# Stacked scores and DMA placing of rotated parts in the second and third branch of a three-mixer trunk

## What is computed

```python
ang = positions[:, :, None, None] * inv_freq
cos, sin = jnp.cos(ang), jnp.sin(ang)
t1, t2 = t[..., :half], t[..., half:]
return jnp.concatenate([t1 * cos - t2 * sin, t2 * cos + t1 * sin], axis=-1)
...
s = jnp.einsum('bqhmd,bkhmd->bhmqk', qi, k) * scale       # head size 64
prob = jax.nn.softmax(jnp.where(mask, s, NEG), axis=-1)
```

## Time and profile before

| | |
|---|---|
| Median of 3 runs | 1538.78 us (1537.62 to 1540.23) |
| The profiled execution's own time | 1537.43 us |
| Its span, first to last instruction | 1535.6 us |
| Busy: PE, PEld (weight loads) | 1496.2 us (97%), 1203.1 (78%) |
| Busy: DVE, ACT, POOL | 936.3 (61%), 634.8 (41%), 74.4 (5%) |
| Mean granted clock of TensorE | 0.997 |
| Bytes moved by DMA | 129.50 MB |

### The profile page before, as it was taken

One profiled execution on the slowest core, in us unless ns is written; L12 is line 12 of the kernel. 1 busy time (PEld: TensorE's weight loads), 2 busy tenths in 40 slices (PEclk: granted clock), 3 DMA queues, 4 the chain that ended last, 5 costly groups with the idle time before them and its releaser, 6 DMA issues.

```text
span 1535.6 us, 22532 instructions
## 1 busy us (share of the span) xinstructions
PE 1496.2 (97%) x7957; PEld 1203.1 (78%) x7957; DVE 936.3 (61%) x2197; ACT 634.8 (41%) x1499; POOL 74.4 (5%) x80
## 2 busy tenths in 40 slices
PE   8999999999999999999999999999999999999997
PEld 6777777777787777888787787787887877778885
DVE  6866755655557766454576667655555567754544
ACT  6434434333344444343444334334334444434343
POOL 1000000000000010000100000000000000000011
PEclk9999999999999999999999999999999999999998
DMA  7233322222223332332342334222222233233321
GB/s 198 83 83 90 97 76 62 56 70 62 69 63 96 91 82 83 103 105 71 106 108 69 103 83 112 60 53 66 63 62 76 69 96 88 71 101 98 89 86 72
DMA packets 250302, 129.50 MB, mean 84 GB/s; under 512 B 45691, under 2 KB 245973, under 8 KB 250197
## 3 DMA queue, kind: packets, MB, share of 16 engines
q1 hardware_dynamic: 250196, 128.13, 31.4%
HBM read 118.67 MB, written 2.10 MB: 79 GB/s over the span
## 4 chain that ended last, share of the span: by engine, by line
PE 87%; DVE 7%; ACT 3%; issue 2%; DMA 0%; SPq 0%; ACTq 0%; DVEq 0%
PE D L744 24%; PE D L746 22%; PE D L745 22%; PE Ob L932 7%; PE S L891 5%; PE T L910 4%; DVE w_lo L1299 2%; ACT w_hi L1062 1%; PE Mb L948 1%; ACT probs L1178 1%; DVE v_b L1394 1%; PE Mb L858 1%; PE Ob L936 1%; PE Mb L825 1%; DMA raw<-in_w_in_dram 0%
## 5 line engine op out<-in xcount | busy, mean ns | idle before, releaser
L744 PE MATMUL D<-h_hi,w_hi 128*128 128x512 f32 x1264 | 544.5, 431 | 10.1 <-DVE zs L1450 3.8
L746 PE MATMUL D<-h_lo,w_hi 128*128 128x512 f32 x1264 | 496.4, 393 | 0.0
L745 PE MATMUL D<-h_hi,w_lo 128*128 128x512 f32 x1264 | 494.4, 391 | 0.0
L1299 DVE TENSOR_TENSOR w_lo<-raw,w_hi 128x512 fp32r<-128x512 f32 (+2 forms) x504 | 293.0, 623 | 295.1 <-ACT w_hi L1062 294.8
L1062 ACT ACTIVATE w_hi<-raw 128x512 fp32r<-128x512 f32 (+2 forms) x504 | 262.8, 569 | 292.3 <-PE D L746 290.0
L744 PEld LDWEIGHTS D<-h_hi,w_hi 128*128 128x128 f32 x1264 | 238.3, 189 | 71.3 <-issue 20.5
L1178 ACT ACTIVATE probs<-probs,nmax 128x128 f32<-128x128 f32 (+3 forms) x256 | 142.0, 556 | 361.4 <-DVE nmax L1551 361.3
L746 PEld LDWEIGHTS D<-h_lo,w_hi 128*128 128x128 f32 x1264 | 237.2, 188 | 53.2
L745 PEld LDWEIGHTS D<-h_hi,w_lo 128*128 128x128 f32 x1264 | 239.3, 189 | 30.3 <-issue 0.5
L1551 DVE CUSTOM_DVE_ANT_0 probs<-S,maskb 128x128 f32<-128x128 f32 (+3 forms) x256 | 115.1, 487 | 45.6 <-PE S L891 28.7
L542 DVE COPY pT<-T 128x128 f32<-128x128 f32 (+3 forms) x160 | 77.6, 487 | 61.5 <-PE T L910 60.8
(11 more groups left out here) (245 smaller groups left out, 1491.7 us busy)
## 6 DMA issues: line engine op xcount, KB each, us to landing
raw<-in_w_in_dram SPq DMA_DIRECT2D x124, 512.0 KB, 3.9
raw<-in_w_in_dram SPq DMA_DIRECT2D x32, 256.0 KB, 3.7
raw<-in_w_out_dram SPq DMA_DIRECT2D x16, 512.0 KB, 4.2
raw<-in_w_ple_gate_dram SPq DMA_DIRECT2D x16, 512.0 KB, 4.3
rs<-rx SPq DMA_DIRECT2D x80, 64.0 KB, 2.0
raw<-in_cmp_w_k_dram SPq DMA_DIRECT2D x8, 512.0 KB, 3.7
raw<-in_cmp_w_v_dram SPq DMA_DIRECT2D x8, 512.0 KB, 3.8
raw<-in_w_br_a_dram SPq DMA_DIRECT2D x16, 256.0 KB, 2.9
```

Of the source, the lines that this page charges most:

```text
L744: pe.matmul(o, w_hi[:, sl, cs], hi[:, k, :], start=(k == 0), stop=False)
L745: pe.matmul(o, w_lo[:, sl, cs], hi[:, k, :], start=False, stop=False)
L746: ins = pe.matmul(o, w_hi[:, sl, cs], lo[:, k, :], start=False, stop=last)
L1299: TT(w_lo[:, sl, half], raw[:, ring(L, t, RAW), half], f(w_hi[:, sl, half]), ALU.subtract).then_inc(M["dve_lo"], 1)
```

## The change

**Scores.** In B and C the two parts of a query head are stacked: `q_st[b][h]` holds hi on one half of the partitions and lo on the other, and the keys hold each part twice, once on each half. One matmul over 128 rows then gives q_hi·k + q_lo·k for one part of k, and two of them a whole score (with lo·lo, which was left out before). A block is four matmuls over 128 rows where it was six over 64. A's scores stay as they were. TensorE now waits for the maxima of the two heads singly.

**Placing.** The rotation's result no longer goes straight to the arena. The sum is kept in `rc` and the swapped copy in `rs`, which lie side by side as `rcs`: POOL multiplies in place in `rs`, ScalarE writes hi over `rs`, VectorE writes lo over `rc`. A new item `put`, 12 groups behind the tile's end (17 for `kwb`), lets SyncE copy the parts to their places with four DMAs: queries 64 x 512 each, keys 64 x 1024. For it SyncE waits for the lo part, and for the scores that used the place (for `kwb` the hidden layer's last tile, whose input lay there). TensorE waits for the placing at a unit's first scores. The next rotation's swap waits for the last placing.

**Moves.** VectorE's x · cos stands in `rot` and no longer at `end`. `vsb`, `kwb` and `za 3` change places in the fourth stage. The value block `vbd` has memory of its own and is cleared once at the start by POOL.

```diff
-    st[3] = [("qb", 0), ("w1v", 0), ("kwb", 0), ("w1v", 1), ("za", 3), ("w1v", 2), ("vsb", 0), ("w1v", 3), ("vwb", 0)]
+    st[3] = [("qb", 0), ("w1v", 0), ("vsb", 0), ("w1v", 1), ("kwb", 0), ("w1v", 2), ("za", 3), ("w1v", 3), ("vwb", 0)]
...
                 follow.append([11, ("rot", t)])
+                follow.append([17 if kind == "kwb" else 12, ("put", t)])
...
+        def places(kind, n):
+
+            if kind[0] == "q":
+                return [(q_st[n % 2][h][half((h + part_) % 2), :], rcs[half(h), part_ * S:(part_ + 1) * S])
+                        for h in range(2) for part_ in range(2)]
+            at = {"ksb": KS, "kwb": KW, "kc": KC[n % 2]}[kind]
+            return [(part(at + 2 * h, 2)[half(g), :], rcs[half(h), :]) for h in range(2) for g in range(2)]
+
+        def place(M, eng, t):
+
+            kind, n, _ = tiles[t]
+            eng.wait_ge(M["qk_s"], rots.after(t))
             if kind == "kwb":
-                return kw_hi, kw_lo, None
...
+                eng.wait_ge(M["pe_dense"], tile_of[("w1v", 3)] + 1)
+            elif kind != "ksb":
+                eng.wait_ge(M["pe_s"], rows_before[(4 if kind == "qb" else 8) + n - 1])
+            for dst, src in places(kind, n):
+                eng.dma_start(f(dst), src).then_inc(M["put_s"], 16)
...
                             if n > 1:
-                                sp.wait_ge(M["pool_rot"], n - 1)
+                                sp.wait_ge(M["put_s"], put_before[tiles[it[1]][:2]])
...
-                            pool.tensor_tensor(rb[:], rs[:], sinT[:], ALU.mult).then_inc(M["pool_rot"], 1)
...
+                            pool.tensor_tensor(rs[:], rs[:], sinT[:], ALU.mult).then_inc(M["pool_rot"], 1)
...
+                            else:
+                                at = {"c": KC[u % 2], "sel": KS, "win": KW}[m]
+                                for h in range(2):
+                                    pe.wait_ge(M["dve_max"], r - 1 + h)
+                                    qx = q_st[b][h][:, qs]
+                                    pe.matmul(Sc[h][:, 0:n], qx, part(at + 2 * h)[:, 0:n], start=True, stop=False)
+                                    pe.matmul(Sc[h][:, 0:n], qx, part(at + 2 * h + 1)[:, 0:n], start=False, stop=True).then_inc(M["pe_s"], 1)
...
                             dve.wait_ge(M["pool_rot"], r)
+                            TT(rc[:], (qf if tiles[t][0] == "qb" else rx)[:], cosT[:], ALU.mult).then_inc(M["dve_rm"], 1)
                             dve.wait_ge(M["dve_rm"], r)
-                            TT(rc[:], rc[:], rb[:], ALU.add).then_inc(M["dve_rs"], 1)
+                            TT(rc[:], rc[:], rs[:], ALU.add).then_inc(M["dve_rs"], 1)
                             dve.wait_ge(M["act_rot"], r)
-                            TT(lo_, rc[:], f(hi_), ALU.subtract).then_inc(M["qk_s"], 1)
+                            TT(new_lo, rc[:], rs[:], ALU.subtract).then_inc(M["qk_s"], 1)
```

More of the change, by code:

```diff
@@ L309, in hybrid_trunk @@
                 hids.add(kind)
-        elif it[0] == "rot":
-            qk_ready.add(tiles[it[1]][:2])
+        elif it[0] == "put":
+            placed.add(tiles[it[1]][:2])
         elif it[0] in ("vt", "gates", "ht", "kcmp", "vcmp", "cs", "ct", "Y"):
@@ L401, in hybrid_trunk, with half @@
         w_lo = sb("w_lo", [P, SPL, 8 * P], F32R)
-        at_arena = -(-nc.sbuf_base // 32) * 32
         arena = sb("arena", [P, 16 * S], F32R)
-        vbd = nc.alloc_sbuf_tensor_at("vbd", [P, 2, P], F32, offset=at_arena + 12 * S * 4)
         def part(n, k=1):
             return arena[:, n * S:(n + k) * S]
-        q_hi, q_lo = [part(0), part(1)], [part(2), part(3)]
-        k_hi, k_lo = [part(4), part(5)], [part(6), part(7)]
-        ks_hi, ks_lo, kw_hi, kw_lo = part(8), part(9), part(10), part(11)
+        def half(h):
+            return slice(HD * h, HD * h + HD)
+        q_hi, q_lo = [part(0), part(2)], [part(1), part(3)]
+        k_hi, k_lo = [part(4), part(6)], [part(5), part(7)]
+        q_st = [[part(2 * b + h) for h in range(2)] for b in range(2)]
+        KC, KS, KW = (4, 8), 8, 12
         flat_both = part(12, 4).rearrange("p (m c) -> p m c", m=16)
@@ L645, in _ @@
                             static_load(it[1] + 6)
+                        if it[0] == "put":
+                            place(M, sp, it[1])
                     sp.wait_ge(M["dve_ysplit"], 12)
@@ L885, in _ @@
                             n = (i + 1) * P
                             qs = slice(i * P, n)
-                            for step, (qx, kx) in enumerate(((q_hi[b], ka), (q_lo[b], ka), (q_hi[b], kb))):
-                                last = step == 2 and m != "a"
-                                for h in range(2):
-                                    ps = slice(HD * h, HD * h + HD)
-                                    ins = pe.matmul(Sc[h][:, 0:n], qx[ps, qs], kx[ps, 0:n], start=(step == 0), stop=last)
-                                    if last:
-                                        ins.then_inc(M["pe_s"], 1)
@@ L894, in _ @@
-                            if m == "a":
-                                for h in range(2):
-                                    ps, hh = slice(HD * h, HD * h + HD), 2 * u + h
+                            if m == "a":
+                                if r >= 2:
+                                    pe.wait_ge(M["dve_max"], r)
+                                for step, (qx, kx) in enumerate(((q_hi, k_hi), (q_lo, k_hi), (q_hi, k_lo))):
+                                    for h in range(2):
+                                        pe.matmul(Sc[h][:, 0:n], qx[b][half(h), qs], kx[b][half(h), 0:n], start=(step == 0), stop=False)
+                                for h in range(2):
+                                    ps, hh = half(h), 2 * u + h
@@ L1166, in _ @@
                             kind, n, s = tiles[t]
-                            hi_, lo_, u = rot_dst(kind, n)
                             act.wait_ge(M["dve_rs"], rots.after(t))
-                            if u is not None and u >= 2:
-                                act.wait_ge(M["pe_s"], rows_before[u - 1])
-                            A(hi_, rc[:], ACT.Copy).then_inc(M["act_rot"], 1)
+                            A(new_hi, rc[:], ACT.Copy).then_inc(M["act_rot"], 1)
                         elif what == "S":
@@ L1450, in _ @@
                                 STT(zs[:], th[:, slot, :], 1.0, Db[:], ALU.add, ALU.mult).then_inc(done, 1)
-                            elif kind in ROTATED:
-                                r = rots.after(t)
-                                dve.wait_ge(M["act_evac"], act_evac.after(t))
-                                if r > 1:
-                                    dve.wait_ge(M["qk_s"], r - 1)
-                                TT(rc[:], (qf if kind == "qb" else rx)[:], cosT[:], ALU.mult).then_inc(M["dve_rm"], 1)
                             elif kind in ("kcb", "vcb"):
```

59 lines of the change are left out of this document (25 added, 34 removed).

## The result

The changed kernel takes 1547.55 us (median of 4 runs, 1546.13 to 1548.74), the kernel before 1539.51 beside it (4 runs, 1537.62 to 1540.61). The ratio is 1.0056, 95% interval 1.0044 to 1.0068: **slower by 0.56%**, where 1519 us and a gain were forecast.

A forecast was written before the change was run, and what follows sets the result against it. The prediction took TensorE as the bound (87% of the chain that ended last). Scores −21.7 and moved multiply +2.4 made −19.3 us, from a median of 1538.8 to 1519.5, stated as 1519 us; range 1511 to 1528.

The forecast's parts named there:

- the placings: Four more DMAs a rotation on SyncE's queue: off TensorE's path, 8 us against 2.5 + 2.5, no cost.
- the moved multiply: VectorE's cosine product in the rotation: two fourth-stage waits grow by 0.6 us each, 2.4 us in two layers.
- the reordering: Fourth stage's new tile order: taken at nothing; 2.6 us more without the half tile's cover, 5.4 less at best.
- The scores: Second and third branch on TensorE: four 128-row matmuls for six 64-row ones save 21.7 us.
- Rivals 1 and 2: Score blocks: all (1556 us, chance 0.04) or half (1536 us, chance 0.05) of the 0.4 us stays.
- the 0.4 us: TensorE's 64-row score blocks: about this much of each is not streaming, at entry, exit and inside.
- rival 1: Score blocks: the 0.4 us belong to leaving the stream, not to 64 rows; 1556 us, slower, chance 0.04.
- Rival 4: TensorE stands at a stage's first scores for a placing; 28 rotations at 1 us each, 28 us; chance 0.02.
- Rival 3: Rotations: placing lands after 3.5 us, the 1.0 us spare is gone, VectorE stands still; 1523 to 1535 us, chance 0.10.
- The clock: Second and third branch: a lower granted clock was listed as a sign of being wrong, with no size.
- Clearing of the value block: At the start on POOL, ahead of the first data: taken as free.
- weight loads behind the placings: SyncE's queue: loads wait 2.46 us behind the placings' issue; 22 us ahead cover 2.5 + 3.9.

The follow-up runs named there:

- e5: The kernel before with only VectorE's product with the cosine moved from the tile's end into the rotation; 1547.47 against 1538.13 us, ratio 1.0058.
- e6: The kernel before with only the fourth stage's tiles in the new order; 1541.84 against 1537.79 us, ratio 1.0021.
- e4: The changed kernel with queries placed unstacked and six 64-row matmuls a score block again; 1561.80 us against 1538.13 for the kernel before, ratio 1.0148.
- e10: The changed kernel with the third branch's swap, rotation and placing three groups earlier; 1573.26 us against 1537.79 for the kernel before, ratio 1.0225.
- e8: The changed kernel with the cosine product back at the tile's end for all 14 rotations; 1533.36 us against 1537.79 for the kernel before, ratio 0.9968.
- e14: The changed kernel with the third branch's swap, rotation and placing two groups earlier; 1545.78 us against 1537.74 for the kernel before, ratio 1.0062.

## Why the prediction was wrong

The forecast was 19.3 us less than before, and the change costs 8 to 9 us. Three terms on the cost side failed: the placings, counted at nothing, cost some 10 us; the moved multiply 9.3 and not 2.4; the reordering 4 and not 0. A fourth step failed with them: the saving of the blocks was carried over whole into the run's time, and 7.5 of its 21.8 us did not arrive.

- **The scores, −21.7 us: right.** Measured block by block it is 24 × (0.20 + 0.21 + 0.27) + 8 × (0.24 + 0.21 + 0.24), the last for the three surroundings of 128 columns, 21.8 us. A matmul of 384 columns, taken at 0.175, came at 0.18. Rivals 1 and 2, by which some of the 0.4 us would have stayed, did not happen, though the run came out on the side of rival 1. The Trainium skill (TensorEngine Tiling (Array Packing), Theoretical Speedup) gives up to twofold for packed contractions of at most 64 rows. By its full factor, an estimate from that page, the six are three passes against four; here the six cost 1.10 us at 512 columns and the four 0.92, so the measurement goes the other way.
- **The moved multiply, +2.4: a step that failed, by 6.9 us.** "In the stages with full dense tiles PE shows no wait there" was read as slack; it was a hand-off without any. Alone it costs 9.3 us (e5). The prediction followed what queues behind the rotation on VectorE. It did not follow ScalarE, whose copy of the sum sits in the middle of the rotation: that copy waits the 0.6 us too, and with it all that is queued on ScalarE. ScalarE's wait for the sum, in before and then in after:

```profile
ACT arena L1171 <- DVE rc L1540: 49.8, 22, 4.4
```

```profile
ACT rcs L1187 <- DVE rcs L1549: 68.8, 28, 4.6
```

  Six rotations that had not been waited for now are. In the fourth stage the wait itself was foreseen about right: PE's idle time grows by 2.9 us, and the 4.3 of e5 come with one half-clock stretch.
- **The reordering, 0 with a bound of 2.6: wrong, the bound too.** "Each tile still has the same half tile behind it" is true and not the point: what counts is which engine empties the bank behind the rotation. 4.05 us (e6), of which about 1 is waits, within the bound, and about 3 the clock behind them. With the multiply in the same place it is 6.5 (e4's fourth stage), less than the 8.3 of the two alone; e4 had two half-clock stretches there, e5 and e6 three between them.
- **The placing, at nothing ("8 us against 2.5 + 2.5"): the largest step that failed**, 9.1 us of waits in after and 11.7 us in C's stages without the stacking. Rival 4, with a chance of 0.02, was the one. Timelines of after, SP, DVE and PE, for one key of C:

```profile
482.22 3.06 SPq L580 DMA_DIRECT2D arena<-rcs  x4
```

```profile
479.39 0.68 DVE L1547 TENSOR_TENSOR rcs<-rx,cosT 128x512 f32<-128x512 f32 x1
480.11 0.69 DVE L1549 TENSOR_TENSOR rcs<-rcs 128x512 f32<-128x512 f32 x1
481.50 0.69 DVE L1551 TENSOR_TENSOR rcs<-rcs 128x512 fp32r<-128x512 f32 x1 [0.70 <-ACT rcs L1187]
```

```profile
486.70 0.39 PE L763 MATMUL D<-y_lo,w_hi 128*128 128x512 f32 x1
488.91 0.33 PE L917 MATMUL S<-arena 128*128 128x128 f32 x1 [1.81 <-DMA arena<-rcs]
```

  The rotation takes from 479.39 to 482.19, the four DMAs are issued by 485.28, and the last lands ahead of 488.91; PE was ready at about 487.1. Three sizes were off. The landing of 256 KB was taken at 2.5 us and is 4.4; the issue of four large ones takes 3.06 us and not 2.46; and the 8 us were counted in PE's groups from the place of the item, while VectorE reaches it late and takes 2.8 us through it. The sizes of after's DMAs (KB each, us from issue to landing):

```profile
arena<-rcs SPq DMA_DIRECT2D x48, 256.0 KB, 4.4
...
arena<-rcs SPq DMA_DIRECT2D x64, 128.0 KB, 2.3
```

- **Rival 3's spare of 1.0 us: right.** POOL's product ended at 478.61 and VectorE came at 479.39:

```profile
477.32 1.29 POOL L716 TENSOR_TENSOR rcs<-rcs,sinT 128x512 f32<-128x512 f32 x1 [16.73 <-DMA rcs<-rx]
```

  It cost nothing. That this is owed to the small size of the query's placing was argued and not shown; e10 shows what it costs once the spare is gone.
- **The clock: there was no term for it**, though a lower granted clock stood among the signs of being wrong. See the last section; 7 to 8 us of the profiled execution of after, and contained in the costs above, not added to them.
- **Clearing of the value block, weight loads behind the placings: right**, as far as PE's waits go. PE's waits for `w_lo` are 1.9 us in both, though those of the weight loads for `w_lo` grew from 11.1 to 13.9 us.

By parts alone: reordering +4, multiply +9.3, together with the placings and nothing stacked +23.7, so some 10 for the placings; stacking −14.3. That gives +9.4 where the ratio says 8.6 with an interval of 6.8 to 10.5. The 10 are a difference and not a part measured alone: with the product back at the tile's end (e8) C's three stages are 1.9 us longer than before, 7.4 more than their blocks' saving allows. Of the stacking's 21.8 us 7.5 are missing. Between the first and the last score block PE is idle for 37.7 us in after and for 34.0 in e4, and after has one half-clock stretch more; that is some 5 us of it in the profiled executions, and the rest is open.

## What to carry to other kernels

A saving on the bound engine arrives only as far as no hand-off becomes late, and a wait that a profile doesn't show may have no slack behind it: follow a moved instruction into every engine that waits in the middle of its chain, and ask of each what is queued behind that wait (here ScalarE, and 0.7 us moved cost 9.3). A wait of some 2 us can cost nearly twice its length when the clock falls behind it, and whether it does differs between runs: count the half-clock stretches before comparing two profiles. Price a placing by DMA from when its producer really ends, with the issue time and the landing of its own size. And place a rotation in the order by which bank must be emptied next: two groups earlier for one branch and two later for one stage turned +0.56% into −0.77% once the product stood back at the tile's end.

## What the runs showed of the hardware

**Half-clock stretches behind long waits.** After a gap of PE of some 2 us, the matmuls often ran at half the rate for 2 to 4 us. Timeline of after, PE:

```profile
205.99 0.47 PE L761 MATMUL D<-h_hi,w_hi 128*128 128x512 f32 x1 [2.48 <-DVE zs L1466]
...
206.76 0.61 PE L761 MATMUL D<-h_hi,w_hi 128*128 128x512 f32 x1
207.17 0.63 PE L762 MATMUL D<-h_hi,w_lo 128*128 128x512 f32 x1
207.59 0.63 PE L763 MATMUL D<-h_lo,w_hi 128*128 128x512 f32 x1
208.02 1.05 PE L930 MATMUL T<-ident,probs 128*128 128x128 f32 x4
208.73 0.77 PE L761 MATMUL D<-h_hi,w_hi 128*128 128x512 f32 x1
...
210.15 0.42 PE L761 MATMUL D<-h_hi,w_hi 128*128 128x512 f32 x1
```

Steps of 0.42 us and more in place of 0.23, and 1.05 us for transposes that take 0.60: the lower of the two levels, 1.2 GHz and not 2.4. From 206.76 to 210.15 are 3.39 us for six dense matmuls and a block of transposes, 6 × 0.23 + 0.44 = 1.82 at the full clock, so 1.5 us are lost beside the wait's own 2.5. The windows of after (from:to, length, busy time of each engine, granted clock, DMA share, GB/s) have it as well:

```profile
206.00:211.00 5.00, 5.00 (x17) 4.03 (x18) 3.38 (x7) 0.42 (x1) 0.00 (x0) 0.66 0.88 229
488.50:492.50 4.00, 3.59 (x13) 2.92 (x14) 3.86 (x9) 0.85 (x2) 0.00 (x0) 0.70 0.64 177
531.50:536.00 4.50, 4.16 (x23) 3.65 (x24) 4.13 (x11) 0.86 (x4) 0.00 (x0) 1.00 0.69 179
```

Inside the stretch the granted clock reads 0.50 from 206.80 to 210.20 us and 1.00 behind it. Five such stretches in after (from 183, 207, 490, 944 and 1289 us), each behind a wait of 1.8 to 2.5 us, cost 7 to 8 us at 1.5 each.

The price can be read from fourth stages in which PE is idle for the same 5.0 us: 50.2 us without a stretch (e14, first layer), 51.8 with one (after, second layer), 53.3 with two (after, first layer), so 1.5 us each.

Before had none of them, its waits in these stages being 1.42 and 1.29 at the longest. Between the first and the last score block no run has one behind a wait of 1.42 us or less; the shortest wait that had one was 1.56 (e4). A longer wait had one often and not always: a wait of 1.76 us at 530 had none behind it (the third window), nor had that of 2.45 us in the second layer of after, nor waits of 2.12 and 2.48 us in e14's first fourth stage; in e10, with its waits of up to 4.7 us, there were nine, two of them twice as long. What decides is left open.

**Copies within SBUF** take 2.3 us to land for 64 x 512 elements (128 KB) and 4.4 for 64 x 1024 (256 KB), each one of four issued in a row, while a weight load of 512 KB from DRAM took 4.0 in the same run: twice the bytes took nearly twice as long, and a copy of half the bytes of that load took longer than the load. A load of 256 KB took 3.8.
